# Differential attention in one core's transformer kernel: shares left undivided until the head norm, squares of a head summed by query, and two projection tiles computed block by block

## The reference, cut to what matters

```python
DIFF_HEADS = 8          # of 2 x 64 query and key columns and 128 value columns each
def diff_attend(q, k, v, lam, lambda_init, subln_g):
    s = jnp.einsum('bqhtd,bkhtd->bthqk', q, k).astype(jnp.float32) * HEAD_DIM ** -0.5
    p = jax.nn.softmax(s, axis=-1)
    a = (p[:, 0] - lam * p[:, 1]).astype(v.dtype)
    o = jnp.einsum('bhqk,bkhe->bqhe', a, v)
    o = rms_norm(o, subln_g) * (1.0 - lambda_init)        # per head and query, eps 1e-6
    return o.reshape(o.shape[0], o.shape[1], DIFF_HEADS * 2 * HEAD_DIM)
...
    out_l = o_l @ w_out                                   # 1024 x 1024
...
    xl = layer_norm(ALPHA * xl + gt1_l * o_l, ln1_g[i], ln1_b[i])
```

## Time and profile before

| | |
|---|---|
| median of three runs | 1800.58 us (1797.69 to 1800.74) |
| the profiled execution | 1793.73 us |
| its span | 1791.8 us |
| PE busy | 1707.9 us (95%) |
| DVE busy | 1048.4 us (59%) |
| ACT busy | 828.9 us (46%) |
| mean granted TensorE clock | 0.982 of full |
| moved by DMA | 287.74 MB, mean 161 GB/s |
| head loop, head norm and output projection of the changed mixer | from 836.5 us to 938.9 us of the span |

### The profile page before, as it was taken

The page is one execution under the profiler, slowest core; times in us unless marked ns, Lnnn a source line. Parts: engine busy times, 40 slices in busy tenths (PEclk is TensorE's granted clock), DMA queues, the critical chain, the costliest instruction groups (busy, mean ns, idle before and its releaser), DMA issues.

```text
span 1791.8 us, 25040 instructions
## 1 busy us (share of the span) xinstructions
PE 1707.9 (95%) x10358; PEld 1360.5 (76%) x10358; DVE 1048.4 (59%) x1516; ACT 828.9 (46%) x1184; POOL 0.9 (0%) x5
## 2 busy tenths in 40 slices
PE   6989989999999999999898999999999999999996
PEld 2746566877877786897578999899876968777775
DVE  2246655534334454436857666657666657888885
ACT  3344543533223323424536444555444337766764
POOL 0000000000000000000000000000000000000000
PEclk9999999999999999999989999999998999999998
DMA  9312524243434425232023464344322319999982
GB/s 373 127 36 83 205 92 151 82 181 135 143 141 148 183 80 188 72 110 79 1 95 121 160 208 163 127 165 144 116 94 71 126 36 381 339 339 351 346 323 109
DMA packets 42677, 287.74 MB, mean 161 GB/s; under 512 B 4784, under 2 KB 5936, under 8 KB 11200
## 3 DMA queue, kind: packets, MB, share of 16 engines
q1 hardware_dynamic: 42384, 285.97, 43.6%
q10 hardware_dynamic: 144, 0.06, 0.0%
q0 software_dynamic: 32, 0.07, 0.0%
HBM read 285.03 MB, written 1.05 MB: 160 GB/s over the span
## 4 chain that ended last, share of the span: by engine, by line
PE 84%; DVE 9%; ACT 4%; issue 2%; DMA 1%; DVEq 0%; ACTq 0%; SPq 0%
PE ps L486 17%; PE ps L488 16%; PE ps L487 16%; PE ps L2619 5%; DVE WL L471 3%; PE ps L2589 2%; PE ps L533 2%; PE ps L2593 2%; PE ps L2590 2%; PE ps L1442 1%; PE ps L1413 1%; PE ps L1344 1%; PE ps L511 1%; DMA ring<-wts 1%; PE ps L613 1%
## 5 line engine op out<-in xcount | busy, mean ns | idle before, releaser
L486 PE MATMUL ps<-HH,WH 128*128 128x512 f32 (+2 forms) x1488 | 496.5, 334 | 17.9 <-DVE WL L471 10.2
L471 DVE TENSOR_TENSOR WL<-ring,WH 128x2048 fp32r<-128x2048 f32 (+2 forms) x191 | 413.4, 2171 | 163.8 <-ACT WH L461 163.3
L488 PE MATMUL ps<-HH,WL 128*128 128x512 f32 (+2 forms) x1488 | 485.0, 326 | 0.0
L487 PE MATMUL ps<-HL,WH 128*128 128x512 f32 (+2 forms) x1488 | 484.6, 326 | 0.0
L461 ACT ACTIVATE WH<-ring 128x2048 fp32r<-128x2048 f32 (+2 forms) x191 | 346.7, 1817 | 207.3 <-DMA ring<-wts 77.4
L486 PEld LDWEIGHTS ps<-HH,WH 128*128 128x128 f32 x1488 | 285.4, 192 | 69.5 <-issue 33.3
L488 PEld LDWEIGHTS ps<-HH,WL 128*128 128x128 f32 x1488 | 285.4, 192 | 22.0
L487 PEld LDWEIGHTS ps<-HL,WH 128*128 128x128 f32 x1488 | 285.8, 192 | 21.0 <-issue 0.5
L486 PE MATMUL ps<-parts,WH 128*128 128x512 f32 (+1 forms) x352 | 119.7, 340 | 0.0
L487 PE MATMUL ps<-parts,WH 128*128 128x512 f32 (+1 forms) x352 | 118.4, 336 | 0.0
L488 PE MATMUL ps<-parts,WL 128*128 128x512 f32 (+1 forms) x352 | 118.3, 336 | 0.0
(11 more groups left out here) (349 smaller groups left out, 2232.7 us busy)
## 6 DMA issues: line engine op xcount, KB each, us to landing
ring<-wts SPq DMA_DIRECT2D x206, 1024.0 KB, 5.0
arena<-wts SPq DMA_DIRECT2D x38, 1024.0 KB, 6.5
ring<-wts SPq DMA_DIRECT2D x32, 704.0 KB, 4.0
X<-xin SPq DMA_DIRECT2D x4, 512.0 KB, 8.8
cst<-csts SPq DMA_DIRECT2D x1, 1373.0 KB, 15.4
ring<-wts SPq DMA_DIRECT2D x3, 384.0 KB, 3.1
out<-arena SPq DMA_DIRECT2D x2, 512.0 KB, 2.9
ring<-wts SPq DMA_DIRECT2D x1, 640.0 KB, 3.5
```

What stands on the lines that cost most here:

```text
L471: e.tensor_tensor(lo, raw(i), hi.bitcast(F32), ALU.subtract).then_inc(*up("low", i))
L486: e.matmul(o, w[0][:, cols], x[0], start=k == 0, stop=False)
L487: e.matmul(o, w[0][:, cols], x[1], start=False, stop=False)
L488: return e.matmul(o, w[1][:, cols], x[0], start=False, stop=k == nk - 1)
```

## The change

Five edits.

1. Undivided shares. `dve_diff_scale` no longer divides both softmaxes by their sums. It keeps the first exponential as it is and adds the second times one factor, minus lambda times the first row sum over the second (a reciprocal and one small operation on two columns, and one 128x512 operation for each query tile, L1748 of the changed kernel). The head comes out multiplied by its first row sum z, by query, and the norm takes it out again: the factor of a head and query is 1 / sqrt(mean of squares + 1e-6 z²).
2. Both PSUM copies of the transposed shares are ACT's (`act_diff_turn`); `dve_diff` has none.
3. Sums by query. `pe_head_sum` makes, for each query tile, a product with the squares as the stationary operand and one column of 1/128 as the moving one, so that the sums of all heads lie in 16 columns of 128 partitions, in two parts (heads 0 to 5, heads 6 and 7). Root and reciprocal run over 12 and 4 columns; those of the first part stand inside the loop (i of 9 and 10), with the table load of the root at i = 8. The spreads take the factor column as a broadcast stationary operand and the identity as the moving one, two products of 128 columns for each head. DVE now issues the product of head h before the lower part of head h-1.
4. Tiles 0 and 1 of the projection are computed together, block by block (`pe_out_pair`, `two_tiles` with `by_k`): for each k three passes of tile 0, then three of tile 1. The norm's sums move behind later tiles: row of means behind tile 2, its spread behind tile 3, then `{4: (3,), 5: (4, 5), 6: (6,), 7: (7,)}`.
5. The second weight chunk of the projection has its lower part made at the end of the inputs (`dve_low(e, index["dout", 0])` between the last rotary turn and lambda); `act_high` at the same place issues nothing, since both upper parts are there already.

```diff
+        def pe_out_pair(e, key, src, arrive, n, tag):
+            c = index[key + (0,)]
+            bs = [bank(e, "out", key, m) for m in range(2)]
+            two_tiles(e, c, weights(e, c), [ps[:, b, 0:n] for b in bs], src, key + (0,), True, (arrive,))
+            for m in range(2):
+                banks.give(bs[m], "y", tag, m)
...
-                        pe_out_sums(e, N, j)
+                        for d in {2: (1,), 3: (2,), 4: (3,), 5: (4, 5), 6: (6,), 7: (7,)}[j] if pair else (j,):
+                            pe_out_sums(e, N, d)
...
             rope("kept.qd", Qd, 7)
+            dve_low(e, index["dout", 0])
...
+            for part in range(2):
+                e.wait_ge(*at("diff_weighed.head", part))
+                for h in HEADS[part]:
+                    b = bank(e, "spread", h)
+                    for qt in range(2):
+                        t = e.matmul(ps[:, b, 128 * qt:128 * qt + 128], weight[:, qt, h:h + 1].to_broadcast([128, 128]),
+                                     ident, start=True, stop=True)
...
+        def act_diff_turn(e, j):
+            if j >= 2:
+                e.wait_ge(*at("diff_values", j - 2))
+            for qt in range(2):
+                e.wait_ge(*at("diff_turned", j, qt))
+                e.activation(*diff_turned(j, qt), ACT.Copy).then_inc(*up("diff_p", j, qt))
...
             for qt in range(2):
-                i = c0 + 2 * qt
-                e.tensor_scalar(P3[z][:, qt, :], P3[z][:, qt, :], es[:, i + 1:i + 2], None,
-                                ALU.mult).then_inc(*up("diff_weighed.second", j, qt))
-                e.wait_ge(*at("diff_weighed.second", j, qt))
-                e.scalar_tensor_tensor(out=PAD[:, z, qt, :], in0=PAD[:, z, qt, :], scalar=rv[:, i:i + 1],
-                                       in1=P3[z][:, qt, :], op0=ALU.mult, op1=ALU.add).then_inc(*up("diff_weighed", j, qt))
+                e.scalar_tensor_tensor(out=PAD[:, z, qt, :], in0=P3[z][:, qt, :], scalar=c[:, qt:qt + 1],
+                                       in1=PAD[:, z, qt, :], op0=ALU.mult, op1=ALU.add).then_inc(*up("diff_weighed", j, qt))
...
-            e.matmul(ps[0:8, banks.of["head_sums",], 0:256], C("strip8")[:, 7 - h:15 - h], SQ1, start=h == 0,
-                     stop=h == 7).then_inc(*up("head_sum", h))
+            for qt in range(2):
+                t = e.matmul(ps[:, b, 8 * qt + h:8 * qt + h + 1], SQ1[:, 128 * qt:128 * qt + 128], C("o128", 1), start=True,
+                             stop=True)
+            t.then_inc(*up("head_sum", h))
```

More of the change, by code:

```diff
@@ L1602, in pe_diff @@
             pe_head_sum(e, 7)
-            e.wait_ge(*at("inverse.head"))
-            for h in range(8):
-                b = bank(e, "spread", h)
-                e.matmul(ps[:, b, 0:256], ident[0:8, h:h + 1].to_broadcast([8, 128]), SQ1[0:8, :], start=True,
-                         stop=True).then_inc(*up("spread", h))
-                banks.give(b, "od_unit", h)
+            for part in range(2):
[5 more added lines that the diff above has]
+                                     ident, start=True, stop=True)
+                    t.then_inc(*up("spread", h))
+                    banks.give(b, "od_unit", h)
         def act_diff(e):
```

100 lines of the change are left out of this document (63 added, 37 removed).

## The result

| | before | after |
|---|---|---|
| median, run on one chip | 1799.13 us (4 runs) | 1783.21 us (4 runs, 1782.83 to 1783.91) |
| ratio of after to before | | 0.9913, 95% interval 0.9896 to 0.993 |
| profiled execution, its span | 1793.73, 1791.8 us | 1783.91, 1782.1 us |

The forecast was 1792.6 (1789.6 to 1797.6). The direction was right; the gain was larger than forecast and the time lies outside the range.

A forecast was written before the change was run, and what follows sets the result against it. PE was taken to bound the loop and the paired projection tiles. Shifts through fill, loop, drain, norm and pair, less a wait in the projection, left 8.1 us, taken as 8.0: 1800.6 - 8.0 = 1792.6 us, range 1789.6 to 1797.6.

The forecast's parts named there:

- Fill: Start of the stage: DVE's first row maximum 2.2 us later, scores of head 4 1.0 us later.
- Steady heads: Loop over heads: PE bounds it at 6.4 us a head, three heads 19.2; scores of head 7 0.55 behind.
- The sum by query: PE's four one-column passes a head in the loop: 0.5 us, bounds 0.4 to 1.1.
- Drain: After the last scores: values of head 7 at 894.4 instead of 895.19, 0.8 us ahead.
- Head norm: After values of head 7: first scaled head at 898.5 instead of 902.99, 4.5 us ahead.
- Pair: Projection tiles 0 and 1: heads every 0.76 us instead of 1.30, end at 907.65 instead of 917.07, 9.4 ahead.
- the new wait: Rest of the projection: PE waits for y4 and its square, losing 1.3 us, bounds 0.3 and 2.5.
- Clock: TensorE runs at 2.4 GHz for the spreads and the pair; lower clock in the fill costs nothing.
- rivals A and B: Lower clock in the norm, 1795 to 1799.7 us, chance 0.13; lower clock through the loop, 1810, chance 0.03.
- C: Loop: ACT's copies come late and PE waits for them in steady heads; 1795.1 us, chance 0.04.
- Rival D: No wait in the projection and PE's sums at their lower bound: 10 us won, 1790.6, chance 0.1.
- Behind 940: Rest of the kernel after the projection: order and size unchanged, so all shifts by the 8.0 us won.

The follow-up runs named there:

- e5: Kernel after with the undivided shares undone (shares divided again, norm limit the constant 1e-6): 1788.23 us.
- e6: Kernel after with undivided shares undone and the copy of the first transposed tile back on DVE: 1790.18 us.
- e12: Kernel before with the undivided shares alone, norm limit kept at 1e-6: 1791.18 us.
- e2: Kernel after with the output projection as before (tiles 0 and 1 not paired, norm's sums where they were): 1782.99 us.
- e16: Kernel before with only the undivided shares and the head norm with sums by query: 1782.63 us.
- e7: Kernel after with DVE's old order in the head norm (lower part of each head before the next head's scaling): 1786.86 us.
- e3: Kernel after without the early lower part of the projection's second weight chunk: 1783.82 us.
- e9: Kernel after, unchanged, run again as control: 1782.75 us.
- e10: Kernel after with the early lower part of the second weight chunk moved on DVE behind the scaling of head 6: 1782.45 us.
- e1: Kernel before, unchanged, run again as control: 1795.28 us.
- e8: Kernel before with 13 unused products of 512 columns added on TensorE in the gap ahead of the head norm's spreads: 1796.85 us.
- e15: Kernel before with 13 unused products ahead of the spreads and two more ahead of each later spread, one fewer at two existing places: 1804.18 us.
- e11: Kernel after with 12 unused products of 512 columns added on TensorE in the fill, ahead of head 1's scores: 1784.64 us.

## Why the forecast was wrong

- **Fill**: right. Forecast 2.2 and 1.0 late, measured 2.1 and 0.8.
- **Steady heads**: the step that failed. "So PE bounds the loop at 6.4", with DVE's 1.6 a head worth 0.15. PE's own work is 5.11 a head: by the starts of the rows scores 1.91, values 1.84, sum 0.36, transposes 1.00. The forecast's 2.96 for the scores held about one us of waits for banks, and before the change DVE set the pace. Three heads took 16.55, not 19.2, and the scores of head 7 were 2.3 ahead instead of 0.55 behind. Shown by e5, e6 and e12: edits 1 and 2 are worth 7.1 us. The clue stood in the forecast's own sentence, that DVE had next to no idle time in these 6.55. The forecast's 6.43 a head "by the differences of the starts" also took 2.96, the length of the score row; from its start to that of the next row it is 2.89.
- **The sum by query**: taken as 0.5 (bounds 0.4 to 1.1); its four passes cost 0.36 from start to start (862.60 to 862.96), 0.09 each, below the lower bound and 0.14 a head less than taken. The 0.136 of the earlier trace rows stood beside products of 8 columns. The Trainium skill (TensorE: Matmul & The Clock Gate, LDWEIGHTS) gives 0.107 for such a load, and this trace is nearer to it than to the row that I took.
- **Drain**: 0.8 ahead forecast, 4.1 measured. Of the 3.3 more, 2.9 are there at the scores of head 7 already, so they are the loop's; the rest is the drain's own.
- **Head norm**: right. Its own part, from the values of head 7 to the first scaled head, shrank by 3.67; forecast 3.7.
- **Pair**: the rate of the heads (0.76 forecast, 0.73 measured) and the new wait (1.3 forecast, 1.25 measured) were right. From the first scaled head to the read of tile 7 it takes 31.56 instead of 35.41, 3.9 won where 3.6 was forecast. That the pair carries the gain was not argued separately from the order on DVE, and it doesn't: e2 and e16 lose nothing without it, e7 loses 3.8 without the order.
- **Clock**: 2.4 GHz through norm and pair was right, so rivals A and B did not come; The sign named for C came, as PE waits for ACT's copy 0.25 in every second head, but its loss did not. In this profile the clock also stayed at 1.00 from 886 to 899, with transposes and one-column products between the values, and through the drain of e3, e9 and e10 alike. In the nine other profiles with the new norm the lower clock came just there, behind the last scores, and ended ahead of the spreads; the values of e16 show it (timeline of PE):

```profile
882.39 3.58 PE L1770 MATMUL ps<-arena 128*128 128x256 f32 x8 [2.24 <-ACT arena L1647]
```

So one and the same mix of transposes and values is seen at both levels, and the rule of the Trainium skill that the forecast weighed (the same page, Part 4: PE-mode transpose) is neither borne out nor refuted here. The forecast took the stretch of one profile for the rule.
- **Rival D** (more is won) had the right sign at 0.1. Of its two reasons one failed, as the wait in the projection came all the same; the sums were cheaper, by 0.14 a head, and most of what the loop won was in neither.
- **Behind 940**: all was to shift alike. It didn't quite: of 11.0 us ahead at 940 the span keeps 9.7, 0.6 of it lost between 965 and 1000. The cause is not traced.
- **The base**: the forecast took 8.0 off the 1800.58 of three runs; 96 runs of the kernel before have 1796.25. Against that base 8.0 is 1788.2, and 13.2 was measured. Between the profiled executions it is 9.8, as the profiled one before was among its quicker ones and e1's stage was 5.7 longer. In size, then, 4.3 of the miss of 9.4 is the base, which has nothing to do with the change. Of the other 5.1, 1.8 is what the profiled pair shows over 8.0 (3.3 more at the values of head 7, less what was lost at the start and behind 940). The other 3.3 is that the profile before lies 2.5 under the median of its 96 runs and the profile after 0.8 over its own. That the loop's error has a part in those too is likely, as edits 1 and 2 are worth 7.1 in medians (e6), but it isn't shown.

What stays open: what sets the 5.5 a head of the changed loop, in which neither DVE (17.13 of 20 busy) nor ACT (13.53 of 20) is full and PE still waits about 1.2 in every second head; and why the old norm's kernels had 10 to 14 us of lower clock in spreads and first tiles in all six of their profiles, while none of the thirteen profiles of kernels with the new norm had any there. Filling the idle time ahead of it did not remove it (e8), nor did wide products between the spreads (e15). How much of edit 3's 8.0 this is could not be separated.

## What to carry to other kernels

When an engine's row is longer than the same instructions elsewhere, look under it (weight loads, their releasers) before calling it that engine's work; a busy share can hide waits for PSUM banks. If another engine had no idle time over a period, it sets the period, and what leaves it is won until something else limits. Read the base from many runs, and price an edit by having it alone and by taking it away alone: three of five edits here were worth nothing that shows once the other two stood.

## What had not been expected of the hardware

The lower clock comes in spells that move between executions of one kernel: in the stage 13.7 us of it in one profile of the kernel before and 27.3 in another. In e15 one began after TensorE had been busy without a break from 905 to 911. Products added to keep TensorE busy left spells in e8, e11 and e15 and shortened the run in none. Eight passes of 64 rows and 512 columns take 1.99 when their banks are free, four passes of one column with 128x128 weights 0.36.
